# Computing the mLSTM gates between the projections' copies, and idle identity products ahead of three waits of TensorE

## The reference, cut to what matters

```
EVEN_SPLIT = [ML_W, ML_W, ML_HEADS * ML_DV, ML_HEADS * ML_DV, 2 * ML_HEADS, 2 * ML_HEADS,
              MLA_Q_RANK, MLA_KV_RANK, MLA_ROPE]
q, k, v, o, ig, fg, cq, ckv, kpe = split_cols(y, EVEN_SPLIT)
logi = ig + P['ml_i_bias'][e]
logf = jax.nn.log_sigmoid(fg + P['ml_f_bias'][e])
b = jnp.cumsum(lf, axis=-1)
dmat = jnp.where(tril, b[..., :, None] - b[..., None, :] + li[..., None, :], -jnp.inf)
mq = jnp.maximum(inter, jnp.max(dmat, axis=-1))
```

## Time and profile before

| | us |
|---|---|
| median of 3 runs | 1463.62 |
| fastest and slowest run | 1461.95, 1466.84 |
| the profiled execution | 1467.7 |
| its span in the trace | 1465.3 |
| mean granted clock of TensorE in it | 0.943 |
| TensorE busy | 1300.8 (89%) |
| VectorE busy | 508.0 (35%) |
| ScalarE busy | 357.6 (24%) |

### The profile page before, as it was taken

The page is one execution under the profiler, slowest core; times in us unless marked ns, Lnnn a source line. Parts: engine busy times, 40 slices in busy tenths (PEclk is TensorE's granted clock), DMA queues, the critical chain, the costliest instruction groups (busy, mean ns, idle before and its releaser), DMA issues.

```text
span 1465.3 us, 16887 instructions
## 1 busy us (share of the span) xinstructions
PE 1300.8 (89%) x6386; PEld 796.3 (54%) x6386; DVE 508.0 (35%) x1061; ACT 357.6 (24%) x755; POOL 112.3 (8%) x136
## 2 busy tenths in 40 slices
PE   6999788989997998788899998989889999978893
PEld 3554675456795333333456555879788843323332
DVE  3010474322225111001364952767782421110014
ACT  2100313433212111111134422433352211111111
POOL 2400010000000111110000001000000011111100
PEclk9999888999998999999998999999999899998997
DMA  9951666356528999999533210010035579999971
GB/s 366 326 199 62 225 139 230 115 194 249 185 91 326 372 387 418 418 418 411 214 98 115 93 51 0 1 30 2 1 116 215 203 291 401 417 418 418 418 295 56
DMA packets 80725, 329.10 MB, mean 225 GB/s; under 512 B 18383, under 2 KB 19577, under 8 KB 55936
## 3 DMA queue, kind: packets, MB, share of 16 engines
q1 hardware_dynamic: 66224, 300.54, 52.8%
q0 software_dynamic: 14416, 27.41, 5.6%
HBM read 320.04 MB, written 29.53 MB: 239 GB/s over the span
## 4 chain that ended last, share of the span: by engine, by line
PE 65%; DMA 15%; DVE 11%; issue 5%; ACT 1%; SPq 0%; POOL 0%; DVEq 0%; ACTq 0%; POOLq 0%
PE psum L929 20%; PE psum L1274 12%; PE psum L1023 8%; DMA ring<-in_moe_w_up 5%; PE psum L1300 5%; DMA arena<-in_moe_w_up 4%; PE psum L955 3%; DMA wide<-in_moe_w_up 3%; PE psum L1018 2%; DMA ring<-in_ada_w 2%; DVE arena L2416 2%; DVE wide L2376 1%; PE psum L898 1%; PE psum L1257 1%; PE psum L962 1%
## 5 line engine op out<-in xcount | busy, mean ns | idle before, releaser
L929 PE MATMUL psum<-wide,ring 128*128 128x384 f32 x704 | 240.5, 502 | 4.3 <-ACT wide L1601 1.9
L929 PEld LDWEIGHTS psum<-wide,ring 128*128 128x128 f32 x704 | 165.7, 239 | 71.0 <-issue 9.9
L1274 PE MATMUL psum<-arena 128*64 128x512 f32 x480 | 149.2, 615 | 18.7 <-DMA ring<-in_moe_w_up 13.4
L1274 PE MATMUL psum<-ring,arena 128*64 128x512 f32 x384 | 138.0, 638 | 10.5 <-DMA ring<-in_moe_w_up 5.7
L929 PE MATMUL psum<-ring,wide 128*128 128x512 f32 (+2 forms) x336 | 118.2, 514 | 0.0
L2287 DVE TENSOR_TENSOR arena<-arena,psum 128x256 f32<-128x256 f32 x34 | 14.3, 422 | 287.2 <-ACT arena L1749 287.2
L1274 PEld LDWEIGHTS psum<-arena 128*64 128x64 f32 x480 | 46.2, 142 | 95.7 <-issue 95.6
L1274 PE MATMUL psum<-wide,arena 128*64 128x512 f32 x224 | 88.1, 610 | 5.8 <-DMA arena<-in_moe_w_up 5.8
L1023 PE MATMUL psum<-arena 128*128 128x128 f32 x608 | 87.4, 296 | 6.4 <-DVE arena L2021 2.6
L929 PEld LDWEIGHTS psum<-ring,wide 128*128 128x128 f32 x336 | 60.4, 199 | 57.2 <-issue 56.4
L1749 ACT ACTIVATE arena<-psum 128x256 f32<-128x256 f32 x34 | 13.1, 384 | 321.0 <-PE psum L1274 321.0
(11 more groups left out here) (512 smaller groups left out, 1741.1 us busy)
## 6 DMA issues: line engine op xcount, KB each, us to landing
ring<-in_ada_w SPq DMA_DIRECT2D x23, 2048.0 KB, 13.1
arena<-in_moe_w_gate SPq DMA_DIRECT2D x28, 1024.0 KB, 14.0
arena<-in_moe_w_up SPq DMA_DIRECT2D x28, 1024.0 KB, 18.7
arena<-in_moe_w_down SPq DMA_DIRECT2D x28, 1024.0 KB, 22.8
ring<-in_moe_w_gate SPq DMA_DIRECT2D x24, 1024.0 KB, 12.9
ring<-in_moe_w_up SPq DMA_DIRECT2D x24, 1024.0 KB, 18.7
ring<-in_moe_w_down SPq DMA_DIRECT2D x24, 1024.0 KB, 20.9
ring<-in_w_in_odd SPq DMA_DIRECT2D x7, 2048.0 KB, 9.1
```

The lines of the kernel that those rows point to most:

```text
L929: ins = mm(out, lhs(k), rhs(k), start=(k == 0), stop=(k == n - 1))
L1274: ins = mm(psum[half, 2 + s, :].rearrange("p (w f) -> p w f", w=2), hg[s][:, k, half], buffers[UNITS[q][h] % BUFFERS][0][:, :, k, :], star ...
```

## The change

Three edits. VectorE computes the bias sums and `log_inputs` directly after the three copies of ta; then it copies tb 0, then waits for ScalarE's logarithms and finishes `log_decay`, and only then copies tb 1, tb 2 and cols. In the second and third steps of the scan (pair 1 and 2) TensorE takes the bank of the first MR job ahead of the wait for `neg_m`, and makes 14 and 4 idle identity products into it before it waits. Ahead of the wait for the copy of kpT, in kpR's bank, it makes 8.

```
                 beside("MR", 2 * pair)
-                pe.wait_ge(S("neg_m"), pair + 1)
                 for u, d, c in two:
-                    spread(issue("MR", u), lambda h: nmr[:, d, h:h + 1])
+                    b = issue("MR", u)
+                    if pair and u % 2 == 0:
+                        keep_busy(b[:, 0:P], 14 if pair == 1 else 4)
+                    pe.wait_ge(S("neg_m"), pair + 1)
+                    spread(b, lambda h: nmr[:, d, h:h + 1])
...
             b = issue("kpR")
+            keep_busy(b[:, 0:P], 8)
             pe.wait_ge(*taken("kpT"))
...
             for c in range(TILES):
                 dve.wait_ge(*computed("ta", c))
                 take(v.tensor_copy(tail[:, c, 0:512], bank("ta", c)), "ta", c)
-            for c in range(TILES):
-                dve.wait_ge(*computed("tb", c))
-                take(v.tensor_copy(tail[:, c, 512:TAIL], bank("tb", c)[:, 0:TAIL - 512]), "tb", c)
             dve.wait_ge(S("small_in"), SMALL)
-            dve.wait_ge(*computed("cols"))
-            take(v.tensor_copy(colsT[:], bank("cols")[:, 0:P]), "cols")
-            done(v.tensor_copy(mln[:, 1].rearrange("p d h -> p (d h)"), colsT[:, 120:128]), "n_start")
-
             for d in range(2):
                 o_(tt(li[:, d], ...
                 o_(tt(lf[:, d], ...
             done(stt(tf, lf, -1.0, lf, ALU.mult, ALU.max), "log_inputs")
             o_(ts(lf, lf, 0.0, None, ALU.min))
-            dve.wait_ge(S("logarithms"), 1)
-            done(tt(lf, lf, tf, ALU.subtract), "log_decay")
+            for c in range(TILES):
+                dve.wait_ge(*computed("tb", c))
+                take(v.tensor_copy(tail[:, c, 512:TAIL], bank("tb", c)[:, 0:TAIL - 512]), "tb", c)
+                if c == 0:
+                    dve.wait_ge(S("logarithms"), 1)
+                    done(tt(lf, lf, tf, ALU.subtract), "log_decay")
+            dve.wait_ge(*computed("cols"))
+            take(v.tensor_copy(colsT[:], bank("cols")[:, 0:P]), "cols")
+            done(v.tensor_copy(mln[:, 1].rearrange("p d h -> p (d h)"), colsT[:, 120:128]), "n_start")
+
```

## The result

The first seven timed executions of the changed kernel have a median of 1455.96 us (1447.25 to 1462.24), against 1463.96 (1461.95 to 1471.76) for the kernel before: ratio 0.9918, 95% interval 0.9891 to 0.9946. The two medians are 8.0 us apart, as forecast (7.7), but the ratio stands for 12.0 us (7.9 to 16.0), or 1452.0 us, and a second comparison of the same kernel gave 0.9925 (0.9900 to 0.9950), 11.0 us. The question is which term was too small.

The account below looks back on a forecast made before the run. The prediction read 65% of the span as hanging on TensorE, 15% on transfers, 11% on VectorE. Terms -8.1 - 0.8 + 0.9 + 0.3 = -7.7 us against the median of 1463.62 gave 1455.9 us, range 1452.5 to 1461.0.

Parts of the forecast that it names:

- The gates, -8.1: From the projection's tail to the first step's MR: earlier gates start MR 8.4 us earlier, less 0.3 for later exponentials.
- The bound of 1.58 us for cum: First step: cum's start to VectorE's copy, 1.58 us at half clock as upper bound; 1.0 taken at full clock.
- The 14 products, -0.8: Second step's wait of 3.70 us: 14 idle products fit in it and keep MR at full clock, gaining 0.8 us.
- The 4, +0.9: Third step, ahead of MR: no wait hides the 4 idle products, so they cost 0.9 us.
- The 8, +0.3: Ahead of kpR: the shared bank delays the 8 idle products, L955 may run faster; net cost 0.3 us.
- the bound of 2.4: Upper bound at the turned keys: 2.4 us lost if the 8 run at half clock; L955 may not gain.
- the signs: Marks expected if right, among them every later mark, such as the output projection's first product, 7 to 8 us earlier.
- Rival A: Gap before R in the first step: the shorter gap still drops the clock, losing 1.7 us; 1457.6 us, chance 0.28.
- B: All three idle groups: they run at half clock and become the wait, costing 5.6 us; 1461.5 us, chance 0.09.
- C: Wherever TensorE comes earlier: ring loads or experts' weights set the pace and swallow the gain; about 1463.6 us, chance 0.07.
- D: Dense product stretches: the shifted program meets more half-clock spells and turns slower, from 1468.0 us; chance 0.04.
- E: Second step: the 14 hold no clock, 0.8 us less gain; 1456.7 us, chance included in the forecast's 0.52.

Follow-up runs that it names:

- e1: Only the gates' edit on the kernel before, no idle products: median 1454.74 us, ratio 0.9920 to the kernel before.
- e7: The whole change, with VectorE reading the modulation vector that shares kpR's bank ahead of its wait for the roots: 1454.53 us, ratio 0.9911 to the kernel before.
- e12: Gates' edit and the 14, plus 4 idle products between the modulation vector's transposition and L955: 1456.93 us, ratio 0.9932 to the kernel before.
- e2: Only the three groups of idle products on the kernel before, gates unchanged: median 1467.45 us, ratio 1.0015 to the kernel before.
- e5: The whole change without the 4 idle products of the third step: median 1458.13 us, ratio 0.9954 to the kernel before.
- e9: Gates' edit and the 14 idle products only, neither the 4 nor the 8: median 1456.02 us, ratio 0.9930 to the kernel before.
- e6: The whole change without the 8 idle products ahead of the turned keys: median 1454.51 us, ratio 0.9911 to the kernel before.
- e3: The changed kernel once more, for a second profile and more times: median 1453.92 us, ratio 0.9925 to the kernel before.
- e8: The whole change, with the scan's one-column products made 128 columns wide: median 1457.97 us, ratio 0.9921 to the kernel before.
- e10: Gates' edit and 7 idle products in place of the 14, neither the 4 nor the 8: 1453.40 us, ratio 0.9919 to the kernel before.
- e4: The kernel before against itself, nothing changed, for a second profile and the scatter: median 1465.13 us, ratio 0.9993.
- e11: Gates' edit and the 14 only, with the scan's one-column products made 128 columns wide: 1452.15 us, ratio 0.9901 to the kernel before.

## Why the prediction was right or wrong

**The gates, -8.1.** Right, step by step. Predicted against the changed kernel's rows, counted from the end of ta's last copy (0.6 us earlier in this execution): the copy ends at 148.51, ScalarE starts 1.1 later, both logarithm functions take 3.2, cum follows at 5.9 (6.1 predicted), R at 7.8 (7.9), MR at 13.6 (13.7; 22.05 before). B grew by 0.2, where 0.3 was charged: the table load begins 0.56 behind MR, and VectorE then waits 0.46 us for ScalarE's last exponentials (L1649). A and B together: -8.3. The bound of 1.58 us for cum was not needed. By the Trainium skill, page "ScalarE: Activation LUTs", section "What ACT_TABLE_LOAD costs", two switches of table would have ended the logarithms near 156, the prediction's estimate from that page. This case's trace doesn't agree: both loads with their functions took 3.2 us, from 149.62 to 152.78.

**The 14 products, -0.8.** This is the step that failed, by its size, as far as the profiles can place it. MR at full clock is worth 0.8, as predicted (2.05 us here, 2.94 before). But the term looked at MR alone. C fell from 20.23 and 18.34 to 16.55 in both profiles of the change, 2.7 us on average. Only 0.75 of it lies between MR and the first product behind the scores; 2.0 lie behind that, where the half-clock spell behind the denominators of the second step was also gone. I had the spell in front of me, as a rival that turns the sign, and not as something that the edit could remove. Over the nine profiles with gates and 14 products C averages 17.0, against 19.3 in the three without: 2.3 us. That it is the idle products is supported by e1 (19.45), not proved in each execution: e7 and e12 have spells there with 14, and e2, with the 14 and without the gates' edit, has a shorter one (17.72). In whole executions the term can't be seen: the gates alone, without the 14, were timed at 11.7 us, as much as the whole change.

**The 4, +0.9.** D grew by 0.9 as predicted. e5 and e9 show that only 0.43 of it is the products: with the second step at full clock TensorE arrives early and would wait about 0.5 us. The reason given, that nothing hides them, was half right.

**The 8, +0.3.** The mechanism was right and e7 shows it: the shared bank holds them until VectorE's reading at L1921. E is 34.4 on average before, 35.1 in the change: +0.7 in the place of +0.3, from two profiles each, which differ by 1.8 and 2.3 us. Against the 33.03 of e6 the two profiles of the change lose 0.9 and 3.2 us, one of them beyond the bound of 2.4. The 8 ran partly at half clock in the change, e3 and e8 (3.0 to 3.3 us for 16 records), and what L955 did behind them varied: full clock in the change and in e8 (3.81, 3.84), half clock in e3, e2 and e5 (5.05 to 6.25). My +0.3 is a mean of such cases, and no run stands for it.

**The sum.** A to E is 106.9 before (mean of two) and 97.5 in the change (mean of two): -9.5, where -7.7 was predicted. 1.9 of the difference are C, the term of the 14, with small errors of the others around it. The attention's first score product, 291.43 in the first profile of before, came at 280.29, 11.1 us earlier, where the signs named 7 to 8. From there to the end nothing is changed. The change's two profiles are 9.3 and 5.1 us shorter there than the first profile of before, but 3.7 shorter and 0.5 longer than the second (1200.1 and 1204.3, against 1209.4 and 1203.8). Over all profiles this last part took 1205.6 us on average in the eleven with the gates' edit (1200.1 to 1212.1) and 1206.9 in the three without it, so no gain clear of scatter is seen there. The 11 to 12 us of the ratios thus hold 9.5 that are placed and about 2 that are not. For the gates alone it is 7.2 placed of 11.7. The intervals reach down to 7.5 to 8 us, so scatter can be all of it; it stays open.

**The rivals.** Rival A, the clock dropping in the shorter gap, did not happen in any of eleven profiles with the gates' edit: the first segment is 13.5 to 13.6 us in all. B happened at the 8 only, in part. C is refuted: the time fell by 11 to 12 us, and from the first transposition of hmT to the attention's first score product it took 35.5 us in twelve of the fourteen profiles, with the gates' edit and without (38.8 in e9 and 37.2 in e12). Of D nothing was seen; the spells moved, and were not more: the mean granted clock is 0.951 over the 94 timed executions with the gates' edit, 0.943 over the 72 before. E, no effect of the 14, is against the rows of C.

## What to carry to other kernels

Look for small operations whose inputs are ready long before their place in a queue: here two table loads and seven small instructions, moved under products, brought 8.5 us with no work saved. Filling a wait with idle products kept the clock behind it where the wait was sure to come and the bank was free, though no whole time here shows a gain by it; check the bank's last reader before the wait's own semaphore, and count the products in records. And when an edit touches the clock, ask what it does to the next weak place too, not only to the instruction behind the wait.

## What the runs showed of the hardware

TensorE's granted clock fell from 2.4 to 1.2 GHz behind products of one column although the engine was never idle: in the kernel before, it had worked without a wait since 200.97, made 32 such records one behind the other between 202.8 and 206.6, and had a grant of 1.00 until 205 and of 0.51 from 206.7 to 212.8. This was so in ten of twelve profiles. Made 128 columns wide, at the same 0.11 us for a record, such products kept the grant at 1.00 over 80 us in both kernels tried.

A wait of 1.95 us left the clock alone in e10, as did the 1.1 us ahead of R in the kernels with the gates' edit, while 3.7 us of waiting cost it in three of three profiles. Ahead of kpR, waits of 2.14 to 4.77 us without the 8 were followed by L955 at 5.08 to 6.59 us, in the place of 3.81, in all seven profiles (before, e4, e1, e6, e9 to e11).
